# Other start addresses for the operands that stream through TensorE

## The chip, the cores and the metric

The kernel runs on one core of a Trainium2 chip, in one launch. The metric is the device time of one execution in microseconds (us).

## The reference

Three blocks run one after the other on 256 tokens of 1024 features, all in float32. Two of them are layers of a first model: a gated feed-forward part with half weight, a mixer (latent attention beside a gated delta rule in the first layer, sparse attention in the second), a second feed-forward part and a gated input from a per-layer embedding. The third is a layer of another model: three mixers whose gated sum is projected back, and a feed-forward part with a squared ReLU. In short:

```
for i in range(2):
    x = x + 0.5 * swiglu(rms_norm(x, ln_ffn1[i]), ffn1_w_gu[i], ffn1_w_down[i])
    x = x + (even_mixer if i % 2 == 0 else odd_mixer)(rms_norm(x, ln_mix[i]), ...)
    x = x + 0.5 * swiglu(rms_norm(x, ln_ffn2[i]), ffn2_w_gu[i], ffn2_w_down[i])
    x = x + sigmoid(rms_norm(x, ln_ple[i]) @ ple_w_gate[i]) * (p[i] @ ple_w_in[i])
x = x + m(rms_norm_2(x, norm1_g)) @ w_out        # m: gated sum of three mixers
x = x + square(relu(rms_norm_2(x, norm2_g) @ mlp_w1)) @ mlp_w2
return rms_norm_2(x, final_g)
```

swiglu(h) is (silu(h @ gate) * (h @ up)) @ down with 2816 inner features; the last feed-forward part has 4096.

## The kernel before, in words

Everything is held feature-major: a tile has 128 features in the partitions and the 256 tokens along the free axis. The kernel runs ten stages in a fixed order (line 30): ffn0, even, ffn1, ple0, ffn2, odd, ffn3, ple1, second, mlp. Weights come as 514 units of 128 x 1024 float32 (512 KB), loaded by SyncE's queue into a ring of three (raw). ScalarE rounds each unit to the short float32 kind that TensorE takes in one pass (w_hi, line 456), VectorE makes the remainder (w_lo, line 464). The activations are split likewise, into h_hi and h_lo or a_hi and a_lo. A product of float32 precision is then three products of short ones, low x high, high x low and high x high, summed in PSUM. All of them are issued by the helper mm at line 475.

In a product one operand is stationary (128 x 128, loaded ahead of it) and one streams past it. Nearly always a weight tile is stationary and the split activation moves:

- h holds the normed input of a stage, eight tiles k of 256 high and 256 low columns side by side. There are two copies: h itself, and h_two, which lies in the arena and is named h_of_feed_forward in the profile. h_of(n) (line 492) picks the copy of a stage: h_two for ffn1, ffn3 and mlp, and for the opening units of even and second; h for the others. up_product (line 496) multiplies a low weight tile by 256 columns of high h and the high tile by all 512 at once; linear (line 507) makes three products of 256.
- a_hi and a_lo hold three rotating tiles of the inner activation. The down projection of a gated feed-forward stage streams them in products of 256 columns, 24 for each of the 22 inner tiles. In the mlp stage, and in two value projections with h, the roles are swapped: the activation is stationary and the weights move, 512 or 256 columns at a time.

Other products (norm sums, attention, the recurrences, transposes) are plain float32, with the arena or the constants as operands.

Engines run their own instruction streams and wait on semaphores; nothing in the order of the work depends on an address. The buffers lie one behind the other in SBUF, each rounded up to 32 bytes. Before the change they begin, in bytes of a partition, at: x 8320, h 16736, raw 33472, w_hi 45760, w_lo 58048, a_hi 70368, a_lo 73440, the parameters 76512, the constants 77920, rstd 91936, the arena 93536, and h_two 32768 behind the start of the arena, 126304. So x and the weights begin at multiples of 64; h, h_two, a_hi, a_lo, the constants, rstd and the arena 32 bytes over one. Every tile of h and of the activations is 1024 or 2048 bytes behind the one before, and so at the same residue.

Of the kernel before, what the change touches and what calls it, by code (L numbers as in the profile page):

```python
# [11 lines left out]
T, P, D = 256, 128, 1024  # L12
KT = D // P
# [41 lines left out]
def offsets(table):  # L55
    out, at = {}, 0
    for name, n in table:
        out[name] = (at, n)
        at += n
    return out, at  # L60
# [226 lines left out]
def build(nc, a_x, a_p, a_w, a_par, a_con, a_gain, out, stages=STAGES):  # L287
    f32 = mybir.dt.float32
    ALU, ACT, AX = mybir.AluOpType, mybir.ActivationFunctionType, mybir.AxisListType
    MUL, ADD, SUB, MAXOP, MINOP = ALU.mult, ALU.add, ALU.subtract, ALU.max, ALU.min  # L290
    par_off, par_n = offsets(PARAMS)
# [7 lines left out]
    with ctx:  # L299
        def sb(name, shape):  # L300
            return ctx.enter_context(nc.sbuf_tensor(name, shape, f32))
# [4 lines left out]
        def sbr(name, shape):  # L306

            return ctx.enter_context(nc.sbuf_tensor(name, shape, mybir.dt.float32r))
# [2 lines left out]

        x = sb("x", [P, KT, T])
        sb("in_front_of_h", [P, 56])
        h = sbr("h", [P, KT, 2, T])
        h_hi, h_lo = h[:, :, 0, :], h[:, :, 1, :]
        sb("behind_h", [P, 88])
        raw = sb("raw", [P, RING, UNIT])
        w_hi, w_lo = sbr("w_hi", [P, RING, UNIT]), sbr("w_lo", [P, RING, UNIT])
        sb("in_front_of_a", [P, 8])
        a_hi, a_lo = sbr("a_hi", [P, 3, T]), sbr("a_lo", [P, 3, T])  # L320
        par = sb("par", [P, par_n + 8])[:, 0:par_n]
        con = sb("con", [P, con_n])
        rstd = sb("rstd", [P, T])
        col_of = sb("second_columns", [P, 11 * 8])
# [1 line left out]
        root_of = sb("roots_of_a_constant", [P, 2 * len(stages) + 2])  # L326
        ps = ctx.enter_context(nc.psum_tensor("ps", [P, 8, 512], f32))
        ARENA = 31981
        with nc.sbuf_tensor("lower_arena", [P, 8192], f32), \
                nc.sbuf_tensor("h_of_feed_forward", [P, KT, 2, T], mybir.dt.float32r) as h_two:  # L330
            pass
        arena = sb("arena", [P, ARENA])

        def f(ap):
# [3131 lines left out]
```

## Time and profile before

| | |
|---|---|
| time, median of 3 runs | 1745.46 us (1744.21 to 1752.84) |
| span of the profiled execution | 1751.1 us, 37772 instructions |
| TensorE busy | 1694.5 us, 97%, 14502 products |
| TensorE weight loads busy | 1574.0 us, 90% |
| VectorE busy | 1290.8 us, 74% |
| ScalarE busy | 995.2 us, 57% |
| DMA | 278.24 MB, mean 159 GB/s |

The span reaches from the first instruction to the last. A product's time in the profile reaches from its start to its modelled end and overlaps that of the next; the pace of a stream is the distance between starts. PE stands for TensorE's products, PEld for its weight loads, DVE for VectorE, ACT for ScalarE.

### The profile page before, as it was taken

To read this page: it belongs to the slowest core of one execution; us is meant where nothing else is said; L and a number is where in the kernel's file an instruction comes from. 1 tells how busy PE (TensorE), PEld (TensorE's weight loads), DVE (VectorE), ACT (ScalarE), POOL (GpSimd) and SP (SyncE) were. 2 spreads that over 40 slices of the span, in tenths; PEclk is the share of its full clock that TensorE was granted. 3 is DMA by queue.
4 is the path that set the end of the run, shared out by engine and by line. 5 is a ranking of instruction groups with operands and counts; after the bars stand their busy time and mean duration, and the time that the engine had idled before them with its cause. 6 is when DMAs were issued, how large, how long until landed. Compare 5 with 4: busy or idle time off the path is not lost.

```text
span 1751.1 us, 37772 instructions
## 1 busy us (share of the span) xinstructions
PE 1694.5 (97%) x14502; PEld 1574.0 (90%) x14502; DVE 1290.8 (74%) x2137; ACT 995.2 (57%) x1562; POOL 3.0 (0%) x9
## 2 busy tenths in 40 slices
PE   7999999999999999999999999989999999899998
PEld 6999899889999989999988999989999998798887
DVE  6777867658777887777767777877788774567776
ACT  5544655445444664445555554668877875444444
POOL 0000000000000000000000000000000000000000
PEclk9999989899999999999999999999999999999999
DMA  6555533115555445554425655545555550055554
GB/s 230 191 188 183 165 133 109 62 31 181 192 191 188 162 166 192 180 191 157 145 82 173 192 188 188 169 157 184 178 183 191 175 163 4 23 174 179 186 187 144
DMA packets 75864, 278.24 MB, mean 159 GB/s; under 512 B 8432, under 2 KB 8688, under 8 KB 75248
## 3 DMA queue, kind: packets, MB, share of 16 engines
q1 hardware_dynamic: 75168, 273.58, 47.9%
q0 software_dynamic: 592, 3.15, 0.5%
q8 instruction: 81, 1.33, 0.3%
q14 instruction: 23, 0.19, 0.0%
HBM read 274.59 MB, written 2.10 MB: 158 GB/s over the span
## 4 chain that ended last, share of the span: by engine, by line
PE 83%; DVE 8%; ACT 6%; issue 2%; DMA 0%; DVEq 0%; SPq 0%; ACTq 0%
PE ps L475 82%; DVE w_lo L464 2%; ACT w_hi L456 2%; PE ps L2471 1%; DVE rstd L607 1%; DVE x L943 1%; DVE h L568 1%; DVE arena L911 0%; DVE arena L915 0%; ACT L2796 0%; ACT L2780 0%; DMA x<-x_t 0%; DVE arena L656 0%; DVE a_lo L931 0%; ACT arena L2133 0%
## 5 line engine op out<-in xcount | busy, mean ns | idle before, releaser
L475 PE MATMUL ps<-h,w_hi 128*128 128x256 f32 (+1 forms) x3380 | 732.4, 307 | 0.0
L464 DVE TENSOR_TENSOR w_lo<-raw,w_hi 128x1024 fp32r<-128x1024 f32 x514 | 621.4, 1215 | 86.6 <-ACT w_hi L456 67.5
L456 ACT ACTIVATE w_hi<-raw 128x1024 fp32r<-128x1024 f32 x514 | 538.6, 1050 | 223.2 <-PE ps L475 205.6
L475 PE MATMUL ps<-h,w_lo 128*128 128x256 f32 x2026 | 583.9, 289 | 22.9 <-DVE w_lo L464 15.6
L475 PEld LDWEIGHTS ps<-h,w_hi 128*128 128x128 f32 x3380 | 554.4, 193 | 26.4
L475 PEld LDWEIGHTS ps<-h,w_lo 128*128 128x128 f32 x2026 | 390.5, 193 | 30.1 <-DVE w_lo L464 14.5
L475 PE MATMUL ps<-h_of_feed_forward,w_hi 128*128 128x512 f32 (+1 forms) x1088 | 351.5, 374 | 0.0
L475 PE MATMUL ps<-h_of_feed_forward,w_lo 128*128 128x256 f32 x1000 | 278.8, 281 | 0.8 <-issue 0.6
L896 ACT ACTIVATE arena<-ps 128x256 f32<-128x256 f32 x208 | 79.1, 382 | 267.7 <-PE ps L475 267.7
L475 PEld LDWEIGHTS ps<-h_of_feed_forward,w_hi 128*128 128x128 f32 x1088 | 198.3, 188 | 36.3
L475 PE MATMUL ps<-a_hi,w_lo 128*128 128x256 f32 x776 | 218.3, 281 | 4.2 <-DVE a_lo L931 4.2
L475 PE MATMUL ps<-a_lo,w_hi 128*128 128x256 f32 x776 | 217.3, 280 | 0.0
L475 PE MATMUL ps<-a_hi,w_hi 128*128 128x256 f32 x776 | 217.0, 280 | 0.0
L911 DVE TENSOR_TENSOR arena<-ps,arena 128x256 f32<-128x256 f32 x208 | 88.3, 424 | 142.3 <-ACT arena L896 141.8
L475 PEld LDWEIGHTS ps<-h_of_feed_forward,w_lo 128*128 128x128 f32 x1000 | 188.2, 188 | 3.3 <-ACT h_of_feed_forward L560 1.2
L475 PEld LDWEIGHTS ps<-a_hi,w_lo 128*128 128x128 f32 x776 | 146.0, 188 | 6.0 <-DVE a_lo L931 5.5
L475 PEld LDWEIGHTS ps<-a_lo,w_hi 128*128 128x128 f32 x776 | 146.1, 188 | 3.2
L475 PEld LDWEIGHTS ps<-a_hi,w_hi 128*128 128x128 f32 x776 | 146.0, 188 | 0.0
L475 PE MATMUL ps<-arena 64*64 64x64 f32 (+6 forms) x2808 | 112.5, 241 | 9.3 <-issue 6.7
L475 PEld LDWEIGHTS ps<-arena 64*64 64x64 f32 (+3 forms) x2808 | 100.0, 147 | 21.3 <-issue 12.5
L915 DVE TENSOR_TENSOR arena<-arena,rstd 128x256 f32<-128x256 f32 x176 | 75.1, 427 | 6.0
L901 ACT ACTIVATE arena<-arena 128x256 f32<-128x256 f32 x120 | 50.1, 418 | 46.2 <-DVE arena L917 33.3
(354 smaller groups left out, 1447.9 us busy)
## 6 DMA issues: line engine op xcount, KB each, us to landing
raw<-weights SPq DMA_DIRECT2D x514, 512.0 KB, 3.4
con<-shape_constants SPq DMA_DIRECT2D x1, 1618.0 KB, 10.5
x<-x_t SPq DMA_DIRECT2D x1, 1024.0 KB, 5.0
stored<-x POOLq DMA_DIRECT2D x1, 1024.0 KB, 4.8
x<-stored POOLq DMA_DIRECT2D x1, 1024.0 KB, 7.9
out_t<-arena SPq DMA_DIRECT2D x4, 256.0 KB, 2.1
arena<-p_t POOLq DMA_DIRECT2D x2, 256.0 KB, 4.1
arena<-final_gain POOLq DMA_DIRECT2D x1, 512.0 KB, 4.6
```

Source lines behind the costliest of these rows:

```text
L456: A.activation(w_hi[:, u % RING, 0:n], raw[:, u % RING, 0:n], ACT.Copy).then_inc(s_hi, 1)
L464: V.tensor_tensor(w_lo[:, u % RING, 0:n], raw[:, u % RING, 0:n], f(w_hi[:, u % RING, 0:n]), SUB)\
L475: return TE.matmul(o, lhsT, rhs, start=start, stop=stop, skip_group_check=True)
L568: last = V.scalar_tensor_tensor(h_[:, k, 1, :], x[:, k, :], G(NORM_OF[stages[n]], k), f(h_[:, k, 0, :]), MUL, SUB)
L607: V.reciprocal(rstd[:, :], rstd[:, :]).then_inc(s_vc, vc.step())
L896: A.activation(rest[:, half, j % f_.bufs, :], ps[:, f_.bank(j) + half, T:2 * T], ACT.Copy).then_inc(s_rest, 1)
L901: A.activation(sg[:, j % f_.bufs, :], tg[:, j % f_.bufs, :], ACT.Silu if f_.gated else ACT.Square).then_inc(s_nl, 1)
L911: V.tensor_tensor((t_, u_)[half], ps[:, f_.bank(j) + half, 0:T], rest[:, half, j % f_.bufs, :], ADD)\
L915: V.tensor_tensor((t_, u_)[half], (t_, u_)[half], rstd[:, :], MUL).then_inc((s_scl, s_fac)[half], 1)
L943: V.scalar_tensor_tensor(x[:, pair_of(b), :], ps[:, b, :].rearrange("p (a t) -> p a t", a=2), 0.5, x[:, pair_of(b), :], MUL, ADD).then_inc ...
L2471: last = TE.transpose(ps[:, bk, s * P:s * P + P], two_heads(src, c, s), ident)
```

## The change

Each of h, h_two, a_hi and a_lo is allocated a little longer and used from a few elements behind its start. h begins 4 elements (16 bytes) later, at 48 over a multiple of 64; the pad behind it shrinks so that raw and the weights stay where they were. a_hi and a_lo begin 2 elements behind the start of buffers that are 64 bytes longer, at 40 over a multiple of 64. The parameters lose their 8 spare elements. Together this moves the parameters by 128 bytes and all that follows them by 96: constants, rstd, the column tables and the arena now begin at the other residue, a multiple of 64 where it was 32 over one and the reverse. The space in front of h_two becomes 64 bytes shorter and h_two begins 4 elements into its buffer, at 16 over a multiple of 64. No instruction and no wait is added or taken away.

```diff
         x = sb("x", [P, KT, T])
         sb("in_front_of_h", [P, 56])
-        h = sbr("h", [P, KT, 2, T])
+        h = sbr("h", [P, KT * 2 * T + 8])[:, 4:KT * 2 * T + 4].rearrange("p (k a t) -> p k a t", k=KT, a=2)
         h_hi, h_lo = h[:, :, 0, :], h[:, :, 1, :]
-        sb("behind_h", [P, 88])
+        sb("behind_h", [P, 80])
         raw = sb("raw", [P, RING, UNIT])
         w_hi, w_lo = sbr("w_hi", [P, RING, UNIT]), sbr("w_lo", [P, RING, UNIT])
         sb("in_front_of_a", [P, 8])
-        a_hi, a_lo = sbr("a_hi", [P, 3, T]), sbr("a_lo", [P, 3, T])
-        par = sb("par", [P, par_n + 8])[:, 0:par_n]
+        a_hi, a_lo = (sbr(name, [P, 3 * T + 16])[:, 2:3 * T + 2].rearrange("p (a t) -> p a t", a=3) for name in ("a_hi", "a_lo"))
+        par = sb("par", [P, par_n])[:, :]
...
-        with nc.sbuf_tensor("lower_arena", [P, 8192], f32), \
-                nc.sbuf_tensor("h_of_feed_forward", [P, KT, 2, T], mybir.dt.float32r) as h_two:
-            pass
+        with nc.sbuf_tensor("lower_arena", [P, 8176], f32), \
+                nc.sbuf_tensor("h_of_feed_forward", [P, KT * 2 * T + 8], mybir.dt.float32r) as h_two_space:
+            h_two = h_two_space[:, 4:KT * 2 * T + 4].rearrange("p (k a t) -> p k a t", k=KT, a=2)
```

## Rows read from the trace of the kernel before

**Rows 1.** The page: busy time and share of each engine; clock by slice.

```profile
PE 1694.5 (97%) x14502; PEld 1574.0 (90%) x14502; DVE 1290.8 (74%) x2137; ACT 995.2 (57%) x1562; POOL 3.0 (0%) x9
PEclk9999989899999999999999999999999999999999
```

**Rows 2.** The chain that ended last: by engine, then its longest pieces (start, us).

```profile
PE 83%; DVE 8%; ACT 6%; issue 2%; DMA 0%; DVEq 0%; SPq 0%; ACTq 0%
...
27.14 167.37 PE ps L475 x1120
...
1571.70 162.29 PE ps L475 x812
```

**Rows 3.** Groups of PE by shape: busy us, mean ns; idle time before them.

```profile
L475 PE MATMUL ps<-h,w_lo 128*128 128x256 f32 x2026 | 583.9, 289 | 22.9 <-DVE w_lo L464 15.6 <-DVE h L652 4.8 <-ACT h L560 1.9
L475 PE MATMUL ps<-h,w_hi 128*128 128x256 f32 x2708 | 497.3, 286 | 0.0
L475 PE MATMUL ps<-h_of_feed_forward,w_hi 128*128 128x512 f32 x912 | 319.9, 392 | 0.0
L475 PE MATMUL ps<-h_of_feed_forward,w_lo 128*128 128x256 f32 x1000 | 278.8, 281 | 0.8 <-issue 0.6
L475 PE MATMUL ps<-h,w_hi 128*128 128x512 f32 x672 | 235.1, 392 | 0.0
L475 PE MATMUL ps<-a_hi,w_lo 128*128 128x256 f32 x776 | 218.3, 281 | 4.2 <-DVE a_lo L931 4.2
...
L475 PE MATMUL ps<-h_of_feed_forward,w_hi 128*128 128x256 f32 x176 | 31.6, 281 | 0.0
```

**Rows 4.** Timeline of PE, up products of ffn0: start us, duration us, moving, stationary.

```profile
105.25 0.28 PE L475 MATMUL ps<-h,w_lo 128*128 128x256 f32 x1
105.36 0.39 PE L475 MATMUL ps<-h,w_hi 128*128 128x512 f32 x1
...
108.71 0.28 PE L475 MATMUL ps<-h,w_lo 128*128 128x256 f32 x1
```

**Rows 5.** Timeline of PE, a down projection of ffn0 and the product behind it.

```profile
94.09 0.28 PE L475 MATMUL ps<-a_hi,w_lo 128*128 128x256 f32 x1
...
96.89 0.28 PE L475 MATMUL ps<-h,w_lo 128*128 128x256 f32 x1
```

**Rows 6.** Timeline of PE, linear units of even, ple0 and second.

```profile
264.04 0.40 PE L475 MATMUL ps<-h,w_hi 128*128 128x256 f32 x2
...
266.18 0.40 PE L475 MATMUL ps<-h,w_hi 128*128 128x256 f32 x2
...
609.16 0.40 PE L475 MATMUL ps<-h,w_hi 128*128 128x256 f32 x2
...
610.60 0.40 PE L475 MATMUL ps<-h,w_hi 128*128 128x256 f32 x2
...
1278.98 0.28 PE L475 MATMUL ps<-h,w_lo 128*128 128x256 f32 x1
...
1280.74 0.28 PE L475 MATMUL ps<-h,w_lo 128*128 128x256 f32 x1
```

**Rows 7.** Timeline of PE at the lower clock; then two stretches by engine, clock behind POOL.

```profile
252.39 0.42 PE L475 MATMUL ps<-h,w_lo 128*128 128x256 f32 x1
...
253.67 0.41 PE L475 MATMUL ps<-h,w_lo 128*128 128x256 f32 x1
...
252.00:254.00 2.00, 2.00 (x12) 2.00 (x11) 1.92 (x9) 1.52 (x3) 0.00 (x0) 0.50 0.74 256
27.00:194.50 167.50, 167.36 (x1122) 154.12 (x1123) 130.47 (x204) 83.34 (x121) 0.00 (x0) 1.00 0.58 187
```

**Rows 8.** VectorE on tiles of x and of the arena; durations, or busy us and mean.

```profile
L1001 DVE TENSOR_TENSOR x<-x,arena x16: 424/424/426, 604.8 to 1147.1; 128x256 f32<-128x256 f32 x16
...
L915 DVE TENSOR_TENSOR arena<-arena,rstd 128x256 f32<-128x256 f32 x176 | 75.1, 427 | 6.0
```

**Rows 9.** Timeline of PE, plain float32 products, one row for several.

```profile
286.29 1.28 PE L475 MATMUL ps<-con,arena 128*128 128x128 f32 x10
...
407.78 1.46 PE L475 MATMUL ps<-arena,con 128*128 128x256 f32 x6
...
1529.52 2.75 PE L475 MATMUL ps<-con 128*128 128x256 f32 x12
```

**Rows 10.** Timeline of PE where weights move: values of odd, then mlp.

```profile
880.80 0.28 PE L475 MATMUL ps<-w_lo,h 128*128 128x256 f32 x1
...
881.88 0.28 PE L475 MATMUL ps<-w_lo,h 128*128 128x256 f32 x1
...
1736.59 0.40 PE L475 MATMUL ps<-w_hi,a_lo 128*128 128x512 f32 x1
...
1740.56 0.40 PE L475 MATMUL ps<-w_hi,a_hi 128*128 128x512 f32 x1
```

## The prediction

> **What bounds the kernel now.** I read the page's busy times first: TensorE (PE) is busy 97% of the span, VectorE 74%, ScalarE 57%, and the granted clock is at its upper level, 2.4 GHz, in most slices [rows 1]. Then the chain that ended last: 83% of it is PE, and its long pieces are unbroken runs of products from line 475, four of 1120 products in 167.4 us (one per gated feed-forward stage) and one of 812 in 162.3 us (the last stage) [rows 2]. So the time is the number of products times their pace, and anything that moves the pace of a product moves the total almost one for one.
>
> The list of groups gives the counts, and its mean durations are not the pace, because products overlap. The streams whose start moves are: from h 2026 + 2708 products of 256 columns and 672 of 512; from the second copy of h 1000 + 176 of 256 and 912 of 512; from the activations 3 x 776 of 256 [rows 3]. That is 5406, 2088 and 2328, together 9822 of 14502 products.
>
> The pace is read from starts in the timeline. In the feed-forward loop ten pairs (256 columns of low weights, then 512 of high weights) take 108.71 - 105.25 = 3.46 us, 346 ns a pair [rows 4]. The 24 products of a down projection take 96.89 - 94.09 = 2.80 us, 117 ns each [rows 5]. The linear units of the mixers, 256 columns each, run at three paces: 15 products in 1280.74 - 1278.98 = 1.76 us (117.3 ns), 18 in 266.18 - 264.04 = 2.14 us (118.9 ns), 12 in 610.60 - 609.16 = 1.44 us (120 ns) [rows 6]. At one column per cycle of 2.4 GHz, 256 columns are 106.7 ns and 512 are 213.3 ns. So a changed product carries about 10 to 13 ns that are not columns, and a pair 26 ns. In a stretch at the lower level, 1.2 GHz, six products take 253.67 - 252.39 = 1.28 us, 213 ns each [rows 7], which is exactly 256 columns: there the extra is gone. So it is something that keeps pace with 1.2 GHz and not with 2.4 GHz: the feeding of the array. The start address can act on that, and on nothing else that I find.
>
> **The change part by part.** No instruction is added, removed or moved, and no wait. Only addresses differ.
>
> (a) Everything behind the activations: two arrays of activations are 64 bytes longer each and the parameter array 32 shorter, so constants, rstd, the column tables and the arena begin 96 bytes later, at another residue of 64 (0 in place of 32). I cost this at nothing on VectorE: operations on x, which begins at a multiple of 64, and on arena tiles, which now begin 32 over one, take 424 to 427 ns alike [rows 8]. On PE: plain float32 products of 256 columns take (1.46 - 0.38) / 5 = 216 ns where the arena moves, at residue 32, and (2.75 - 0.38) / 11 = 215 ns where the constants do, whose tables begin at various multiples of 4 bytes [rows 9]; 256 columns at two cycles each are 213.3, so little is left to lose or win. What hides any VectorE or ScalarE cost is the 97% of PE; without that cover a nanosecond on each of 2137 VectorE instructions would be 2 us.
>
> (b) The three moved streams. No row shows a start at 16, 40 or 48, so the price is bounded from both sides by other rows. The trace has two residues: 32 for h and the activations, and 0 for the weights, which are the moving operand in the last stage's down projection (17 products of 512 columns in 1740.56 - 1736.59 = 3.97 us, 233.5 ns) and in a value projection (9 of 256 in 881.88 - 880.80 = 1.08 us, 120 ns) [rows 10]. Against that, at 32, a 512 takes 346 - 117 = 229 to 230 ns [rows 4, 5] and a 256 takes 117 to 120, middle 118 [rows 5, 6]. So 32 bytes go with about 2 ns per 256 and 3.7 ns per 512. It isn't clean evidence, since the stationary operand changed places too.
>
> Bound above: all changed products at the pace seen for start 0. Pairs 353.5 instead of 346, 1584 of them: +11.9 us. The other 4734 + 1176 - 1584 = 4326 products of 256 at 120 instead of 118: +8.7. The activations at 120 instead of 117: 2328 x 3 = +7.0. Together +27.6 us.
>
> Bound below: the float32 rows show what feeds without stall: 111 ns a product when only weight loads limit it (ten of 128 columns, (1.28 - 0.28) / 9) and 215 ns for 512 cycles [rows 9]. Pairs at 326: 1584 x 20 = -31.7; 4326 x 7 = -30.3; 2328 x 6 = -14.0. Together -76 us.
>
> The value that I take is a straight line through the two residues: bytes further into the 64 make the start cheaper, 1 ns per 256 and 1.85 ns per 512 for each 16 bytes. h gains 16 bytes: 4734 x 1.0 + 672 x 1.85 = -6.0 us. The second copy loses 16: 1176 x 1.0 + 912 x 1.85 = +2.9 us. The activations gain 8: 2328 x 0.5 = -1.2 us. Sum -4.3 us. The profiled execution spans 1751.1 us, 5.6 above the median of the runs, 1745.46; on its own scale that is 1746.8, on the median's 1741.2.
>
> Two rules of the Trainium skill bear on this. "SBUF — State Buffer", section "SBUF: two separate sides", has lines of 16 bytes that run at full rate when a line is hit at least twice. By it 0, 16, 32 and 48 are alike and 40 gives two hits at either end of a stream, so no stream changes: 1745.5, the first rival below. The trace speaks against it only weakly, by the 233.5 and 230 ns of two starts that the rule holds equal [rows 4, 10]. "TensorE: Matmul & The Clock Gate", section "Back-to-back issue gap", estimates N / 2.4 + 2.5 ns for a warm product, 109 and 216 ns; the float32 rows agree (215), the split products of this kernel don't (117 and 230), so by it there is some 75 us to win, near my lower bound.
>
> **The rivals.** *Nothing moves*: all streams shift by a constant, and every product meets the same sequence of line ends. For it: the pace of h alone wanders between 117.3 and 120 with no change of address [rows 6], so residue isn't what sets it. Time 1745.5.
>
> *The stall largely goes*: 32 is a bad phase against the weights, which are loaded from a multiple of 64 beside every product, and off that phase the two reads stop meeting. For it: no stall at 1.2 GHz [rows 7], none in the float32 rows. Against: start 0 for the moving operand, with weights' roles swapped, doesn't shed it [rows 10]. Half of the way to the lower bound for both copies of h, (31.7 + 30.3) / 2 = 31.0 us, and a quarter for the activations, which move only 8 bytes, 14.0 / 4 = 3.5: -34.5 us, 1711.
>
> *Slower: 32 is the best start*, because half a 64-byte piece in front and half behind are what overlaps best between two products, and the cost rises on both sides. The place is each product's start; the price the same 1 and 1.85 ns per 16 bytes, now with one sign: 6.0 + 2.9 + 1.2 = +10.1 us, 1755.6. It decides if h at 48 is slower per product than h at 32; then all three terms have the sign of a loss. If the price is that of the upper bound, 1773.
>
> **How the numbers follow.** Straight line 0.36, nothing 0.14, stall goes 0.28, 32 is best 0.22. Half a per cent, 8.7 us, is about what a measurement of this kernel can tell from no change: faster means below 1736.7, slower above 1754.2. The straight line's own range is 1732 to 1750, some 0.11 of its 0.36 below 1736.7, 0.02 above 1754.2 and the rest between. Nothing: all between. Stall goes: all faster. 32 is best: 0.18 slower, 0.04 between. Faster 0.11 + 0.28 = 0.39, same 0.23 + 0.14 + 0.04 = 0.41, slower 0.02 + 0.18 = 0.20. The range of 1708 to 1764 takes in the middle of both outer rivals; beyond it lie the far half of the second and the tail of the third.
>
> **What would show it.** In the changed profile the pair of a stage fed from h should take 343 ns and that of a stage fed from the second copy 349, where both are 346 now; the down projection 116.5 ns. Equal pairs for both copies, moved the same way, refute the straight line: shorter ones mean the stall went, longer ones that 32 was best. The float32 rows and VectorE's operations on arena tiles should not move; if they do, part (a) is wrong. Waits of PE that grow would show that another engine became late, which I expect nowhere: VectorE is busy 130 us of a 167.5 us feed-forward stretch [rows 7].

## The result and the profile after

The changed kernel takes 1766.59 us (median), the kernel before 1747.26, four runs of each: a ratio of 1.0097, 95% interval [1.0081, 1.0114], which is 17 us slower, 14 to 20 by the interval (the two medians lie 19 apart). That lies above the range of the forecast (1708 to 1764) and on the side that it gave the least chance. The profiled execution spans 1764.7 us, 13.6 more than that of before.

No wait grew: in the page of the changed kernel TensorE (PE) has 14 us more busy time, VectorE and ScalarE the same as before [rows 1], and the chain is PE for 87%.

```profile
PE 1708.7 (97%) x14502; PEld 1584.8 (90%) x14502; DVE 1290.5 (73%) x2137; ACT 995.5 (56%) x1562; POOL 3.0 (0%) x9
...
PE 87%; DVE 7%; ACT 4%; issue 1%; DMA 0%; SPq 0%; DVEq 0%; ACTq 0%
```

The long unbroken pieces of the chain (start, us, products) show where: 1120 products of a gated feed-forward stage took 167.4 us [rows 2] and take 170.1; the last stage took 162.3 and takes 163.3.

```profile
418.49 170.08 PE ps L475 x1120
...
948.31 170.08 PE ps L475 x1120
1584.35 163.26 PE ps L475 x812
```

The paces are read from starts in PE's timeline, as in [rows 4, 5]. The next three rows are of ffn0, fed from h: 16 pairs of 256 and 512 columns from the first row to the second, then 24 down products to the third. The other three are of ffn1, fed from the second copy of h.

```profile
80.34 0.28 PE L475 MATMUL ps<-h,w_lo 128*128 128x256 f32 x1
...
85.93 0.28 PE L475 MATMUL ps<-a_hi,w_lo 128*128 128x256 f32 x1
...
88.82 0.28 PE L475 MATMUL ps<-h,w_lo 128*128 128x256 f32 x1
...
472.47 0.28 PE L475 MATMUL ps<-h_of_feed_forward,w_lo 128*128 128x256 f32 x1
...
478.07 0.28 PE L475 MATMUL ps<-a_hi,w_lo 128*128 128x256 f32 x1
...
480.96 0.28 PE L475 MATMUL ps<-h_of_feed_forward,w_lo 128*128 128x256 f32 x1
```

A pair takes 5.59 / 16 = 349.4 ns from h (349.6 as a mean over the trace) and 5.60 / 16 = 350.0 from the second copy; a down product takes 2.89 / 24 = 120.4 ns, where it took 117 [rows 5]. Before, a pair took 346.7 ns by the mean from either copy; for h see [rows 4], and 16 pairs of the second copy in ffn1 took 5.55 us:

```profile
460.83 0.28 PE L475 MATMUL ps<-h_of_feed_forward,w_lo 128*128 128x256 f32 x1
...
466.38 0.28 PE L475 MATMUL ps<-a_hi,w_lo 128*128 128x256 f32 x1
```

In the linear units the three paces of before [rows 6] have become one: 72 products between these two rows, 8.58 / 72 = 119.2 ns.

```profile
912.70 0.28 PE L475 MATMUL ps<-h,w_lo 128*128 128x256 f32 x1
...
921.28 0.28 PE L475 MATMUL ps<-h,w_lo 128*128 128x256 f32 x1
```

What part (a) of the forecast costed at nothing is unmoved. The first row is VectorE on x and an arena tile, 424 ns as in [rows 8]; the second is twelve float32 products of the constants, 2.75 us as in [rows 9].

```profile
L1001 DVE TENSOR_TENSOR x<-x,arena x16: 424/424/428, 609.9 to 1158.2; 128x256 f32<-128x256 f32 x16
...
1541.78 2.75 PE L475 MATMUL ps<-con 128*128 128x256 f32 x12
```

The sum by stream, from the distance between starts in both traces, product by product, where products follow one another closely (at most 160 ns apart behind 256 columns, 300 behind 512) at the upper clock: pairs from h 2.9 ns each, 1.9 us; pairs from the second copy 3.8 ns, 3.5 us (3.5 ns in ffn1 and ffn3, 4.6 in the last stage); products from the activations 3.5 ns, 8.0 us; linear products from h 1.2 ns, 4.5 us, and 0.2 from the second copy. Together some 18 us. The two profiled executions differ by 13.6: in the same count the wider gaps behind split products, where TensorE waits, are 3.4 us shorter together, and what ran at the lower clock in either trace is 1.0 us shorter. So most of what the streams lose reaches the end of these two executions, and not all of it.

### The profile page after: what moved, and what is told of

Read it like the earlier page. It is cut to its first block, busy times and chain, and to the rows that moved or that the text cites. A ratio compares the mean times of both kernels' runs of the same rounds, so it can differ in the third digit from the quotient of the medians.

```text
span 1764.7 us, 37772 instructions
## 1 busy us (share of the span) xinstructions
PE 1708.7 (97%) x14502; PEld 1584.8 (90%) x14502; DVE 1290.5 (73%) x2137; ACT 995.5 (56%) x1562; POOL 3.0 (0%) x9
## 4 chain that ended last, share of the span: by engine, by line
PE 87%; DVE 7%; ACT 4%; issue 1%; DMA 0%; SPq 0%; DVEq 0%; ACTq 0%
PE ps L475 86%; DVE w_lo L464 2%; PE ps L2471 1%; ACT w_hi L456 1%; DVE rstd L607 1%; DVE h L568 1%; DVE arena L911 0%; DVE x L943 0%; DMA x<-x_t 0%; DVE arena L656 0%; DVE arena L915 0%; ACT arena L2133 0%; DVE a_lo L931 0%; DVE h_of_feed_forward L568 0%; DVE arena L1659 0%
```

## The experiments

All but e15, which starts from the changed kernel, start from the kernel before. They move buffers by pads, or by starting an operand some elements into its buffer; every time is a ratio to the kernel before on the same chip. "Distance" below is the start of the moving operand minus the start of the rounded weights, within 256 bytes, worked out from the allocation; it came in after the first four runs. The kernel before has 160 for both copies of h and 32 for both activations; the changed kernel 176, 208, and 40 and 104 for a_hi and a_lo: because the padded a_hi is 64 bytes longer, a_lo moved by 72 and not by 8.

**e1: h alone at 48.**

```diff
-        h = sbr("h", [P, KT, 2, T])
+        h = sbr("h", [P, KT * 2 * T + 16])[:, 4:KT * 2 * T + 4].rearrange("p (k a t) -> p k a t", k=KT, a=2)
...
-        sb("behind_h", [P, 88])
+        sb("behind_h", [P, 72])
```

> Only h begins at 48; the second copy and the activations stay at 32, constants and arena where they were. If each stream pays for its own start (own start): up products of ffn0 and ffn2 go from 346.7 to 349.6 ns a pair as in the changed kernel, ffn1 and ffn3 stay at 346.7, the linear units settle at 119.25 ns, down projections stay at 116.9; total about +2 to +7 us. If the cost comes from how the streams stand to each other (relation), the pairs of ffn0 and ffn2 or their down projections take another value than in either kernel. If constants and arena cost (elsewhere): all as before.

Ratio 1.0036 [1.0017, 1.0054]. Pairs of ffn0 take 5.59 us for 16, 349.4 ns, linear units 8.59 / 72 = 119.3 ns; ffn1 is as before. h pays for its own move, the same as in the changed kernel.

```profile
898.35 0.28 PE L475 MATMUL ps<-h,w_lo 128*128 128x256 f32 x1
...
906.94 0.28 PE L475 MATMUL ps<-h,w_lo 128*128 128x256 f32 x1
```

**e2: activations alone at 40.**

```diff
-        a_hi, a_lo = sbr("a_hi", [P, 3, T]), sbr("a_lo", [P, 3, T])
-        par = sb("par", [P, par_n + 8])[:, 0:par_n]
+        a_hi, a_lo = (sbr(name, [P, 3 * T + n])[:, 2:3 * T + 2].rearrange("p (a t) -> p a t", a=3)
+                      for name, n in (("a_hi", 16), ("a_lo", 8)))
+        par = sb("par", [P, par_n])[:, :]
```

> Only a_hi and a_lo begin at 40. Own start: down projections of all four gated stages go from 116.9 to 120.3 ns a product, up pairs stay at 346.7 ns, total +7 to +8 us (2112 products x 3.35 ns = 7.1). Relation: down projections return in part towards 116.9, or up pairs change too. Elsewhere: as before.

Ratio 1.0073 [1.0056, 1.009]. The down products of ffn0 take 2.89 / 24 = 120.4 ns:

```profile
85.14 0.28 PE L476 MATMUL ps<-a_hi,w_lo 128*128 128x256 f32 x1
...
88.03 0.28 PE L476 MATMUL ps<-h,w_lo 128*128 128x256 f32 x1
```

That is the loss of the change in its down products. But the pairs of ffn1 and ffn3, whose residue of 64 had not moved, went from 346.7 to 353.4 ns: the pads had carried the arena, and the second copy in it, 64 bytes on. None of the theories had that, and so the time is 13 us longer where 7 to 8 were expected.

```profile
471.01 0.28 PE L476 MATMUL ps<-h_of_feed_forward,w_lo 128*128 128x256 f32 x1
...
476.67 0.28 PE L476 MATMUL ps<-a_hi,w_lo 128*128 128x256 f32 x1
```

**e3: second copy alone at 16.**

```diff
-        with nc.sbuf_tensor("lower_arena", [P, 8192], f32), \
-                nc.sbuf_tensor("h_of_feed_forward", [P, KT, 2, T], mybir.dt.float32r) as h_two:
-            pass
+        with nc.sbuf_tensor("lower_arena", [P, 8184], f32), \
+                nc.sbuf_tensor("h_of_feed_forward", [P, KT * 2 * T + 4], mybir.dt.float32r) as h_two_space:
+            h_two = h_two_space[:, 4:].rearrange("p (k a t) -> p k a t", k=KT, a=2)
```

> Only the second copy of h begins at 16. Own start: pairs of ffn1, ffn3 and the last stage 350.0 ns in place of 346.7, all else as before: 912 pairs x 3.3 ns = +3 us. Relation: another value. Elsewhere: as before.

Ratio 1.0003 [0.9993, 1.0013]. A miss for the own-start theory: 16 pairs take 5.55 us, 346.9 ns (347.3 as a mean over the stage), at the residue at which the changed kernel has 350.0.

```profile
463.21 0.28 PE L475 MATMUL ps<-h_of_feed_forward,w_lo 128*128 128x256 f32 x1
...
468.76 0.28 PE L475 MATMUL ps<-a_hi,w_lo 128*128 128x256 f32 x1
```

**e4: constants and arena moved by 96 bytes, all streams kept at 32.**

```diff
-        par = sb("par", [P, par_n + 8])[:, 0:par_n]
+        par = sb("par", [P, par_n + 32])[:, 0:par_n]
...
-        with nc.sbuf_tensor("lower_arena", [P, 8192], f32), \
+        with nc.sbuf_tensor("lower_arena", [P, 8184], f32), \
...
```

> h, its second copy and the activations stay at 32; constants, rstd and arena move by 96 bytes as in the changed kernel. Own start and relation: no change, under 3 us either way. Elsewhere: +10 us or more.

Ratio 1.0016 [1.0004, 1.0029]. All paces as before but for the second copy, again 32 over a multiple of 64, though 64 bytes on: 5.65 / 16 = 353.1 ns a pair.

```profile
464.34 0.28 PE L475 MATMUL ps<-h_of_feed_forward,w_lo 128*128 128x256 f32 x1
...
469.99 0.28 PE L475 MATMUL ps<-a_hi,w_lo 128*128 128x256 f32 x1
```

So the residue of 64 isn't the variable. The next four ask for the period and for what the start is measured against.

**e5: a_lo alone 64 bytes on; e7: both activations 8 bytes on, a_lo padded to move by 136.**

```diff
-        a_hi, a_lo = sbr("a_hi", [P, 3, T]), sbr("a_lo", [P, 3, T])
-        par = sb("par", [P, par_n + 8])[:, 0:par_n]
+        a_hi, a_lo = (sbr(name, [P, 3 * T + n])[:, 0:3 * T + 0].rearrange("p (a t) -> p a t", a=3)
+                      for name, n in (("a_hi", 16), ("a_lo", 0)))
+        par = sb("par", [P, par_n + 24])[:, 0:par_n]
...              # e7:
+        a_hi, a_lo = (sbr(name, [P, 3 * T + n])[:, 2:3 * T + 2].rearrange("p (a t) -> p a t", a=3)
+                      for name, n in (("a_hi", 32), ("a_lo", 8)))
+        par = sb("par", [P, par_n])[:, 0:par_n]
```

> a_lo alone begins 64 bytes later (a_hi and all else at 32 over a multiple of 64, and a_lo too: its residue of 64 doesn't change); what lies behind moves by 128. Theory of 128: what counts is the start in blocks of 128 bytes, and a_hi and a_lo in different halves cost what e2 showed; down projections near 120 ns a product (116.9 before), total +6 us. Theory of 64 (the residue that the change names): 116.9 ns and no change of time. Moving the second copy of h by 128 should leave its pairs at 346.7 ns by both; if the period is 256 they change.

> Both activations begin 8 bytes later, a_lo padded so that it stays in the same half of 128 bytes as a_hi (both 104 over a multiple of 128). Theory of 128: most of the loss of e2 is gone, down projections 116 to 118 ns. Theory of 64: they stay at 120.4, as in e2, since the residue of 64 is 40 again.

Ratios 0.9999 [0.9985, 1.0013] and 0.9997 [0.9986, 1.0008]. Down products take 2.83 / 24 = 117.9 ns in both; here e7:

```profile
85.24 0.28 PE L476 MATMUL ps<-a_hi,w_lo 128*128 128x256 f32 x1
...
88.07 0.28 PE L476 MATMUL ps<-h,w_lo 128*128 128x256 f32 x1
```

By the means, 64 bytes of a_lo alone cost 1.0 ns (e5), 8 bytes of both with 128 more for a_lo 1.0 ns (e7), and 8 bytes of a_hi with 72 of a_lo 3.8 in e2 and 3.4 in the change. The theory of 64 fails in e7; that of 128 was right there and too high in e5.

**e6: h alone 64 bytes earlier; e11: h alone 64 bytes later.**

```diff
-        sb("in_front_of_h", [P, 56])
+        sb("in_front_of_h", [P, 40])   # e11: 72
-        sb("behind_h", [P, 88])
+        sb("behind_h", [P, 104])       # e11: 72
```

> h alone begins 64 bytes earlier, again 32 over a multiple of 64. Theory of 128: pairs of ffn0 and ffn2 go to 353 ns, as those of the second copy did when it moved by 64 in e4, and the linear units lose 1 to 3 ns a product; +5 to +15 us. Theory of 64: no change.

> h alone 64 bytes later; e6 moved it 64 earlier and had pairs of 349.9. Theory of 128: 349.9 again, linear units 119.9. Period of 256: the second copy's value when it moved 64 later in e4, 353.2; total +5 to +12 us.

Ratios 1.0034 [1.0024, 1.0045] and 1.0021 [1.001, 1.0032]. 64 earlier gives 349.9 ns a pair, not 353, and 8.64 / 72 = 120.0 ns in the linear units; 64 later gives 5.65 / 16 = 353.1. The two lie 128 bytes apart: the period isn't 128. The time of e11, 3.7 us longer, is below the 5 to 12 expected. First 72 linear products of e6, then 16 pairs of e11:

```profile
904.85 0.29 PE L475 MATMUL ps<-h,w_lo 128*128 128x256 f32 x1
...
913.49 0.29 PE L475 MATMUL ps<-h,w_lo 128*128 128x256 f32 x1
```

```profile
80.90 0.28 PE L475 MATMUL ps<-h,w_lo 128*128 128x256 f32 x1
...
86.55 0.28 PE L475 MATMUL ps<-a_hi,w_lo 128*128 128x256 f32 x1
```

**e8: the weights 64 bytes later, h 64 earlier.**

```diff
-        sb("in_front_of_h", [P, 56])
+        sb("in_front_of_h", [P, 40])
...
-        sb("behind_h", [P, 88])
+        sb("behind_h", [P, 104])
...
+        sb("in_front_of_w", [P, 16])
...
-        sb("in_front_of_a", [P, 8])
+        sb("in_front_of_a", [P, 24])
```

> The rounded weights begin 64 bytes later, at a multiple of 128, h 64 bytes earlier; the second copy and the activations stay at 96 over a multiple of 128. If the distance to the weights counts: pairs of ffn0 and ffn2, at the old distance, 346.7 ns, pairs of ffn1 and ffn3 353, down projections about 120. If the place itself counts: pairs of ffn0 and ffn2 353, of ffn1 and ffn3 346.7, down projections 116.9. Theory of 64: all as before.

Ratio 1.0013 [1.0003, 1.0023]. Here h is where e6 had it, but pairs of ffn0 take 347.0 ns in place of 349.9, and the linear units 8.40 / 72 = 116.7 in place of 120.0. The activations, which moved by 128 and so lie 64 further from the weights, take 120.0 a down product. Linear products read h and the weights alone, and h lies as in e6, so it is the weights' move that changed them. ScalarE and VectorE write the weights at their new place too, but that isn't needed for the difference: linear products during which neither engine works take 119.8 ns in e6 (124 products) and 116.7 in e8 (110). One value missed: pairs of ffn1 347.3, where the relation theory had 353 (back to that below).

```profile
908.47 0.28 PE L476 MATMUL ps<-h,w_lo 128*128 128x256 f32 x1
...
916.87 0.28 PE L476 MATMUL ps<-h,w_lo 128*128 128x256 f32 x1
```

**e9: everything behind x moved by 64 bytes.**

```diff
-        sb("in_front_of_h", [P, 56])
+        sb("in_front_of_h", [P, 72])
```

> One edit: the pad in front of h is 64 bytes longer, so h, the weights, the activations, constants and arena all begin 64 bytes later and keep every distance between them; only x stays. If only the distances between the streams and the weights count (relation): all paces as before to 0.1 ns: pairs 346.7, linear units 118.1 on average, down 116.9, and no change of time. If the place itself counts: pairs of ffn1 and ffn3, now where e4 had them, 353 ns, down projections other than 116.9, total +3 us or more.

Ratio 1.0007 [0.9994, 1.002], and every pace as before: pairs 346.7 in all four stages, down 116.9, linear units 118.1 on average. The second copy now lies at the very address that it had in e4, with 353 ns there and 5.54 / 16 = 346.3 here:

```profile
463.84 0.28 PE L475 MATMUL ps<-h_of_feed_forward,w_lo 128*128 128x256 f32 x1
...
469.38 0.28 PE L475 MATMUL ps<-a_hi,w_lo 128*128 128x256 f32 x1
```

So a common move of 64 bytes does not count, and the distances do.

**e10: h alone 128 bytes on; e12: 144 on; e13: 256 on.**

```diff
-        sb("in_front_of_h", [P, 56])
+        sb("in_front_of_h", [P, 88])   # e12: 88, and 4 elements in; e13: 120
-        sb("behind_h", [P, 88])
+        sb("behind_h", [P, 56])        # e12: 40; e13: 24
```

> h alone 128 bytes later. Relation with a period of 256: h stands to the weights as in e8, where it had moved 64 down and the weights 64 up: pairs of ffn0 and ffn2 347.0 ns, linear units 116.9 in place of 118.1, total -3 to -5 us. Theory of 128: pairs 346.7, linear units 118.1, no change. Place: no forecast, but not both of the values of e8.

> h alone 144 bytes later: residue 48 of 64 as in the changed kernel and in e1, but 128 bytes further on. Theory of 64 and theory of 128: pairs 349.8 and linear units 119.2 as in e1, +6 us. Period of 256: other values.

> h alone 256 bytes later. Relation with a period of 256: all paces as in the kernel before, pairs 346.7, linear units 118.1 on average with the levels 117.3, 118.7 and 120.0, down 116.9. A longer period: pairs of ffn0 and ffn2 or linear units at another value.

e10: ratio 0.998 [0.9967, 0.9992], faster than before; pairs 346.6, linear units 8.41 / 72 = 116.8 ns, the pace that e8 had with the same distance of h to the weights and another one to the activations.

```profile
900.34 0.28 PE L475 MATMUL ps<-h,w_lo 128*128 128x256 f32 x1
...
908.75 0.28 PE L475 MATMUL ps<-h,w_lo 128*128 128x256 f32 x1
```

e12: ratio 1.0001 [0.9991, 1.0011]; pairs 349.6 as in e1, linear units 118.3 where e1 had 119.25: each theory missed one of the two. e13: ratio 1.0002 [0.9987, 1.0016]; pairs 346.7, linear units 118.2 on average. So 256 bytes change nothing, 128 change the linear units. In e13, 16 pairs of ffn0:

```profile
79.73 0.28 PE L475 MATMUL ps<-h,w_lo 128*128 128x256 f32 x1
...
85.28 0.28 PE L475 MATMUL ps<-a_hi,w_lo 128*128 128x256 f32 x1
```

**e14: both copies of h 128 bytes further from the weights.**

```diff
-        sb("in_front_of_h", [P, 56])
+        sb("in_front_of_h", [P, 88])
...
-        sb("behind_h", [P, 88])
+        sb("behind_h", [P, 56])
...
-        par = sb("par", [P, par_n + 8])[:, 0:par_n]
+        par = sb("par", [P, par_n + 40])[:, 0:par_n]
```

> Both copies of h 128 bytes later against the weights (e10 for h, and the arena with the second copy as well); activations as before. Relation: h as in e10 (pairs 346.6, linear units 116.9), the second copy's pairs about 347, its few linear units 116.9: -3 to -4 us against the kernel before, no better than e10 by more than 1 us. Against the changed kernel -20 us.

Ratio 0.9977 [0.9962, 0.9992], 1742.13 us against 1747.07: the best version, faster than both kernels, and no better than e10 by more than the interval. Each feed-forward piece takes 167.2 us; the chain's first and last long pieces:

```profile
27.55 167.24 PE ps L475 x1120
...
1560.00 162.11 PE ps L475 x812
```

**e15: the change's residues of 64 in other blocks, shown against the kernel before.**

```diff
+        h = sbr("h", [P, KT * 2 * T + 8])[:, 4:KT * 2 * T + 4].rearrange("p (k a t) -> p k a t", k=KT, a=2)
...
+        a_hi, a_lo = (sbr(name, [P, 3 * T + n])[:, 2:3 * T + 2].rearrange("p (a t) -> p a t", a=3)
+                      for name, n in (("a_hi", 32), ("a_lo", 8)))
+        par = sb("par", [P, par_n + 32])[:, 0:par_n]
...
+        with nc.sbuf_tensor("lower_arena", [P, 8184], f32), \
+                nc.sbuf_tensor("h_of_feed_forward", [P, KT * 2 * T + 4], mybir.dt.float32r) as h_two_space:
+            h_two = h_two_space[:, 4:KT * 2 * T + 4].rearrange("p (k a t) -> p k a t", k=KT, a=2)
```

> All residues of 64 as in the changed kernel (48, 16, 40), but in other blocks: a_lo 64 bytes further on, the second copy at the distance that it had in e3. Relation: pairs 349.7 for h, 347.3 for the second copy, linear units 119.2, down 117.8; total +7 to +9 us against the kernel before, half of the change's loss. Residue of 64: the paces of the changed kernel (349.6, 350.0, 120.3) and +17 us.

Ratio 1.0053 [1.0029, 1.0077]. The residues are 48, 16 and 40 as in the change, and about half of its loss is gone: down products 2.83 to 2.84 us for 24 (118.0 to 118.3 ns), second copy 5.55 / 16 = 346.9 ns a pair; h keeps its 350. The rows are of ffn1:

```profile
467.51 0.28 PE L476 MATMUL ps<-h_of_feed_forward,w_lo 128*128 128x256 f32 x1
...
473.06 0.28 PE L476 MATMUL ps<-a_hi,w_lo 128*128 128x256 f32 x1
...
475.90 0.28 PE L476 MATMUL ps<-h_of_feed_forward,w_lo 128*128 128x256 f32 x1
```

All runs by distance, with paces in ns as means over the trace (pair of 256 and 512, for the second copy in ffn1 and ffn3; linear product; down product):

| kernel | h: distance, pair, linear | second copy: distance, pair | a_hi, a_lo: distances, down |
|---|---|---|---|
| before, e9, e13 | 160, 346.7, 118.1 to 118.2 | 160, 346.7 | 32, 32, 116.9 |
| changed | 176, 349.6, 119.3 | 208, 350.0 | 40, 104, 120.3 |
| e1 | 176, 349.8, 119.2 | 160, 346.7 | 32, 32, 116.8 |
| e2 | 160, 347.3, 117.8 | 224, 353.4 | 40, 104, 120.7 |
| e3 | 160, 346.7, 118.2 | 144, 347.3 | 32, 32, 116.8 |
| e4 | 160, 346.7, 118.2 | 224, 353.2 | 32, 32, 117.0 |
| e5 | 160, 347.0, 118.1 | 32, 347.4 | 32, 96, 117.8 |
| e6 | 96, 349.9, 119.9 | 160, 346.7 | 32, 32, 117.3 |
| e7 | 160, 347.0, 118.2 | 32, 347.1 | 40, 168, 117.8 |
| e8 | 32, 347.0, 116.9 | 224, 347.3 | 96, 96, 120.0 |
| e10 | 32, 346.6, 116.9 | 160, 346.7 | 32, 32, 116.8 |
| e11 | 224, 353.2, 118.3 | 160, 346.7 | 32, 32, 117.0 |
| e12 | 48, 349.6, 118.3 | 160, 346.7 | 32, 32, 116.9 |
| e14 | 32, 346.6, 116.9 | 32, 346.6 | 32, 32, 116.7 |
| e15 | 176, 350.1, 119.3 | 144, 347.1 | 40, 168, 118.2 |

The times follow less exactly than the paces. By this table e6 should lose some 10 us, and its ratio says 6. Its runs had a mean granted clock of 0.986 where those of before on that chip had 0.984, which is 7 us less at the lower level and, at some 213 ns a product there against 118, about 3 us of the difference. So a layout is better read from paces than from a time.

## Why the prediction was wrong, point by point

*What bounds the kernel* held in the main: the streams' paces add up to some 18 us in the two traces, of which 13.6 reach the end of the profiled executions, and the ratio of the runs says 17.

*Part (a)* held for what it priced, VectorE and the float32 products. It missed that the second copy of h rides on the arena: moving it by 64 bytes, and no other stream, costs 6.5 ns a pair in ffn1 and ffn3 (e4). In the changed kernel the pads and the shorter lower arena put it at distance 208, where a pair takes 350.0; at the same residue and distance 144 it takes 347.3 (e3).

*Part (b)*, "a straight line through the two residues", is the step that failed. The start of the moving operand within 64 bytes isn't what sets the pace: at residue 32 a pair takes 346.7, 349.9 or 353.2 ns (before, e6, e11), at residue 16 it takes 347.3 or 350.0. The two rows from which the line was drawn differed in more than the residue, as the text said beside it, and that caution should have stopped the line. By its terms: h was to gain 6.0 us and lost 6.4 (1.9 + 4.5); the second copy was to lose 2.9 and lost 3.7 (3.5 + 0.2), near by luck, for another reason; the activations were to gain 1.2 and lost 8.0, the largest miss. Their edit was read as 8 bytes, and for a_lo it was 72.

*Nothing moves* is refuted by e1 and e2. *The stall largely goes* had the right variable, the phase against the weights, and the wrong sign: distances 160 and 32 were already among the best that the runs found. *32 is the best start* had the right sign and, with its upper price, the nearest time (1773 against 1766.59); its deciding point came out as it said (h at 48 is slower), but its reason falls with e6 and e11, slower at 32, and e3, not slower at 16.

The bound above, 27.6 us, held. The bound below rests on a misread row: its 111 ns "when only weight loads limit it" are float32 products of 128 columns, which at the two cycles a column that the prediction counts for float32 are 106.7 ns of columns, so the row doesn't show what weight loads allow. No run came near that bound; the lowest mean for 256 columns is 116.7 ns (e14). The range ended at 1764 because the upper price had been given little of the chance.

On the two pages: from the Trainium skill, "SBUF — State Buffer", the prediction took lines of 16 bytes and worked out that 16, 32 and 48 are alike; e1 against before has 3 ns a pair between 48 and 32, and e6 and e11 show that even equal starts within 16 bytes differ. The same page of the Trainium skill also states, under "Who interferes with whom", that TensorE's two read ports, one for the moving operand and one for weights, are independent, and under "SBUF: two separate sides" that TensorE never waits on anyone. The runs don't fit that: h lies at one address in e6 and e8 and the weights 64 bytes apart, and its linear products take 120.0 and 116.7 ns. The 109 ns that the prediction worked out for 256 columns from its second page were reached by no split stream here.

What is shown is the dependence on distance. That the stream and the weight load collide in SBUF is a reading that fits; no run here removed the loads, and it is not shown. Open as well: the function itself. The distance doesn't fix the pace alone. The second copy at distance 224 takes 353.2 ns in e4 and 347.3 in e8, though in both it lies equally far from the weights to the byte; of the streams of these stages, what differs is the activations' distance, 32 against 96. Starts repeat with 121, 229, 117, 240 ns in e4 and with 117, 229, 118, 229 in e8, which can be followed here, first e4, then e8:

```profile
465.51 0.40 PE L475 MATMUL ps<-h_of_feed_forward,w_hi 128*128 128x512 f32 x1
465.75 0.28 PE L475 MATMUL ps<-h_of_feed_forward,w_lo 128*128 128x256 f32 x1
465.87 0.39 PE L475 MATMUL ps<-h_of_feed_forward,w_hi 128*128 128x512 f32 x1
466.10 0.28 PE L475 MATMUL ps<-h_of_feed_forward,w_lo 128*128 128x256 f32 x1
```

```profile
473.95 0.39 PE L476 MATMUL ps<-h_of_feed_forward,w_hi 128*128 128x512 f32 x1
474.18 0.28 PE L476 MATMUL ps<-h_of_feed_forward,w_lo 128*128 128x256 f32 x1
474.29 0.39 PE L476 MATMUL ps<-h_of_feed_forward,w_hi 128*128 128x512 f32 x1
474.52 0.28 PE L476 MATMUL ps<-h_of_feed_forward,w_lo 128*128 128x256 f32 x1
```

So one distance allows more than one repeating pattern. That fits the three paces of the linear units before the change [rows 6], at one distance. What chooses the pattern is open. That the products before a unit do is a guess: slow down products alone don't make it, since e2 has 353.4 behind down products of 120.7 ns, and e8 347.3 behind 120.0.

## What to carry to other kernels

This is one kernel; no other was run. In it, where TensorE sets the time, pads in front of operands moved the time by up to 0.7% (e2) and the whole change by 1%: in such a kernel, after any change of layout, compare paces of products by stream, from starts, and not mean durations. Try distances between the moving operand and its weights over 256 bytes rather than alignments, and let every buffer behind a pad keep its distance. Before pricing an edit of addresses, list the address of every operand after it; here the 64 bytes that came with the 8 were the larger edit for a_lo.

## What the runs showed of the hardware

- Paces of short-float products at the upper clock depend on where the moving operand lies relative to the weights: 64 bytes took pairs from 346.7 to 353.2 ns (e11), 128 took linear products from 118.1 to 116.9 (e10), 256 changed nothing (e13), and neither did moving both by 64 (e9).
- In steady state a stream locks into a repeating pattern, with means that come in steps: linear units run at about 117.3, 118.7 or 120.0 ns at one distance (before), at 119 to 119.5 at another (e1), at 119.5 to 120 at a third (e6).
- At the lower clock, 1.2 GHz, a product of 256 columns takes its columns, 213 ns, at distance 160 [rows 7] and at distance 96 alike: in e6 six take 230.25 - 228.97 = 1.28 us, where at the upper clock the distance costs 1.8 ns.

```profile
228.97 0.41 PE L475 MATMUL ps<-h,w_lo 128*128 128x256 f32 x1
...
230.25 0.41 PE L475 MATMUL ps<-h,w_lo 128*128 128x256 f32 x1
```

- Plain float32 products of the constants take 215 ns for 256 columns before and after. Both of their operands moved together, so this shows that their residue doesn't count and says nothing of distance.
